# Second normalisation of a hybrid encoder step: the inverse root applied by VectorE at the take-out of the up-projection, matmuls on x times the norm's weights

## The chip, the core and the metric

The kernel runs on one core of a Trainium2 chip. The metric is the device time of one execution in microseconds, the median of several runs. A core has TensorE (PE), VectorE (DVE), ScalarE (ACT), GpSimd (POOL) and SyncE (SP, which issues the DMAs here). Each engine works through its own instruction list in order, and the lists meet only in semaphores: `wait_ge(s, n)` holds an engine until the semaphore `s` has reached `n`.

## What is computed

Two layers of an encoder for 1024 prompt positions and 32 sample positions (together T = 1056 columns), model width 1024. The attention half of a layer is not touched by the change. The half that matters is:

```python
x = x + o @ w["w_o"]
y, new["conv"] = _conv_ffn(_rms(x, w["norm2_g"]), prev, w["f_win"], w["f_conv_w"], w["f_conv_b"], w["f_wout"])
return x + y, new

def _rms(x, g):
    y = x * lax.rsqrt(jnp.mean(x * x, axis=-1, keepdims=True) + EPS)
    return y * g

def _conv_ffn(h, prev, w_in, cw, cb, w_out):     # w_in: 1024 x 5632, w_out: 2816 x 1024
    up = jnp.concatenate([prev, h @ w_in], axis=1)
    c = cb + up[:, 0:S] * cw[0]
    for j in range(1, CONV_W):                    # CONV_W = 3
        c = c + up[:, j:j + S] * cw[j]
    a, b = jnp.split(c, 2, axis=-1)
    return (jax.nn.silu(a) * b) @ w_out, up[:, S:]
```

The inverse root is one number per position. Since the up-projection is linear, it can be multiplied in before the matmul or behind it, ahead of the convolution.

## The kernel before

x lies transposed in SBUF: `x_t` is 128 partitions by 8 blocks (KC) by 1056 positions. Every large matmul is done in three parts of reduced precision: an operand is split into a high part (a cast, ScalarE) and a low part (the difference, VectorE), and `dense` (L1568) issues high x high, high x low and low x high, each over three bands of 352 positions in three PSUM banks: nine matmuls for one block of weights.

`ffn_block` begins with the second norm. `sumsq` (sums of squares over the blocks) is there already. TensorE turns it into means over the partitions (`norm.mean`, three bands, L302), ScalarE takes the roots (`norm.roots`, L308), VectorE the reciprocals (`norm.inverses`, L314). Then, for each of the 8 blocks, VectorE computes `h = x * weight * rinv` (L333), ScalarE its high part `h_hi` (L319), and VectorE or, for three blocks, GpSimd the low part `h_lo` (L324). TensorE's first two units of the up-projection run jointly along with this, block by block, as `h_lo` comes (`norm.wait_low`).

The rest is a software pipeline over i = 0 to 10 (FG = 11), four up-projection units j = 0 to 3 for each i (8 blocks x 9 matmuls = 72 matmuls each; two units for the half a and two for the half b), and behind them the down-projection `down(i)` of the pass before (8 chunks m of 18 matmuls), which adds to x. i = 0 has no down-projection, and `down(11)` follows at the end alone. The order on each engine is written out by hand in its `body`:

- TensorE: units j = 0 to 3, then `down`. A unit waits for its weights' low part (`lo_done`) and for its banks (`up_copied`). `down` waits for the low part of the second of its two weight tiles, unit number (i, 5).
- ScalarE: for each j, `ahead(i, j, split)` (the cast of the weights two units on, L1969), then `chunk`: four copies take unit j out of PSUM into `up` (L1980 to L1983, one of them puts the saved state in), and one activation begins the convolution in `cv` (L1987). For odd j follow `gate` (Silu, L1993) and `high` (cast of the product, L2001).
- VectorE: for each j, `ahead(i, j, split)` (the low part of the weights two units on, L2042), then `conv` (two instructions, L2048 and L2051), for odd j `multiply` (L2060, L2061) and `low` (L2066), and the eight adds of the down-projection to x (L2072), some of them between these.
- GpSimd saves the last two columns of each unit (L1865), and SP loads the weights (L1838), each load when the split two before it is done.

`ahead` decides what stands where: with six weight tiles (i, 0) to (i, 5) per pass it takes, at step j, the tile j + 2. So `ahead(i, 3, split)` is the split of tile (i, 5), and `ahead(i, 4)` and `ahead(i, 5)` are those of tiles (i + 1, 0) and (i + 1, 1).

Of the kernel before, what the change touches and what calls it, by code (L numbers as in the profile page):

```python
# [23 lines left out]
P = 128  # L24
# [20 lines left out]
def build_program(nc, I, O, consts):  # L45
# [71 lines left out]
    def sem(name):  # L117
        all_sems.append(nc.alloc_semaphore(name))
        return all_sems[-1]

    class S:
# [69 lines left out]
        down_done = sem("down_done")  # L191
        x_added = sem("x_added")
        st_saved = sem("st_saved")
        x_ready = sem("x_ready")
        x_sq = sem("x_sq")
        h_ready = sem("h_ready")
# [1570 lines left out]
    def ffn_block(layer):  # L1767
# [11 lines left out]
        cv = w.take("cv", [P, 2, UPC - 2])  # L1779
        up_flat = up[:, :, :].rearrange("p b c -> p (b c)")  # L1780
        sq = up_flat[:, 0:2 * T].rearrange("p (b c) -> p b c", c=T)
        w = Region(R_V + 4 * T, R_W)
        prod = w.take("prod", [P, T])
        st_t = w.take("st_t", [2 * FC * 2, 2, P])
        norm = Norm(2 * 2 * FC + 8, (6, 7, 5), Region(R_Q, R_V))
        w_sem = (S.w_loaded0, S.w_loaded1)
        win = I["f_win"][layer].rearrange("(k p) (s m c) -> s m p k c", p=P, s=2, c=P)
        wout = I["f_wout"][layer].rearrange("(m p) n -> m p n", p=P)
# [36 lines left out]
        with nc.Block() as block:  # L1825
# [29 lines left out]
            @block.gpsimd  # L1855
            def _(pool):
                pool.memset(up[:, :, 0:2], 0.0).then_inc(S.pool_step, 1)
                norm.pool_low(pool)

                def save(i):  # L1860
                    for q in range(4):
                        c = (q % 2) * FC + 2 * i + q // 2
                        pool.wait_ge(S.up_copied, 4 * i + q + 1)
                        src = up[:, q % 2, SEQ:SEQ + 68].rearrange("p (a b) -> p a b", b=34)[:, :, 0:2]
                        pool.tensor_copy(conv_st[:, :, :, bass.ds(c, 1)], src.unsqueeze(3)).then_inc(S.st_saved, 1)  # L1865

                save(0)
                with pool.Fori(1, FG) as i:
                    save(i)

            @block.tensor
            def _(pe):
                def up_unit(i, j):
                    n, ws, _ = number(i, j)
                    pe.wait_ge(S.lo_done, n + 1)
                    first = kind(i) == "first"

                    if j < 2:
                        if not first:
                            pe.wait_ge(S.up_copied, 4 * i - 1 + j)  # L1880
                            if not (isinstance(i, int) and i == 1):
                                pe.wait_ge(S.x_added, 8 * i - 9 + j)
                    else:
                        pe.wait_ge(S.up_copied, 4 * i + j - 1)
                    for k in range(KC):
                        last = dense(pe, w_hi[:, ws, k * P:(k + 1) * P], w_lo[:, ws, k * P:(k + 1) * P], k, k == 0, k == KC - 1,
                                     h_hi[:, k, :], h_lo[:, k, :], 3 * (j % 2))
                    last.then_inc(S.up_done, 1)

                def down(i, par):  # L1890

                    pe.wait_ge(S.act_lo, 2 * i)
                    for j in (4, 5):
                        n, _, _ = number(i, j)
                    pe.wait_ge(S.lo_done, n + 1)
                    for m in range(KC):
                        if m < 2:
                            if not (isinstance(i, int) and i == FG):
                                pe.wait_ge(S.up_copied, 4 * i + 3 + m)
                            else:  # L1900
                                pe.wait_ge(S.up_copied, 4 * FG - 1 + m)
                                pe.wait_ge(S.x_added, 8 * (FG - 1) - 1 + m)
                        else:
                            pe.wait_ge(S.x_added, 8 * (i - 1) + m - 1)
                        for k in range(2):
                            ws = number(i, 4 + k)[1]
                            last = dense(pe, w_hi[:, ws, m * P:(m + 1) * P], w_lo[:, ws, m * P:(m + 1) * P], k, k == 0, k == 1,
                                         act_hi[:, par, k, :], act_lo[:, par, k, :], 3 * (m % 2))
                        last.then_inc(S.down_done, 1)

                def body(i, par):
                    for j in range(2 if kind(i) == "first" else 0, 4):
                        up_unit(i, j)
                    if kind(i) != "first":
                        down(i, 1 - par)


                norm.mean(pe)
                pe.wait_ge(S.lo_done, 2)
                for k in range(KC):  # L1920
                    norm.wait_low(pe, k)
                    for j in range(2):
                        last = dense(pe, w_hi[:, j, k * P:(k + 1) * P], w_lo[:, j, k * P:(k + 1) * P], k, k == 0, k == KC - 1,
                                     h_hi[:, k, :], h_lo[:, k, :], 3 * j)
                        if k == KC - 1:
                            last.then_inc(S.up_done, 1)
                body(0, 0)
                body(1, 1)
                body(2, 0)
                with pe.Fori(1, (FG - 1) // 2) as pair:  # L1930
                    body(2 * pair + 1, 1)
                    body(2 * pair + 2, 0)
                down(FG, 0)
                for half in range(2):
                    if half == 0:
                        pe.wait_ge(S.st_saved, 4 * FG)
                    last = pe.transpose(ps[0:4 * FC, 6 + half, 0:P], conv_st[:, half, :, :].rearrange("p r c -> p (r c)"), ident[:, :])
                last.then_inc(S.tr_done, 1)

            @block.scalar  # L1940
            def _(act):
# [29 lines left out]
                def chunk(i, j):  # L1971

                    b = j % 2
                    s0 = 3 * b
                    c = b * FC + 2 * i + j // 2
                    act.wait_ge(S.up_done, 4 * i + j + 1)
                    if not (kind(i) == "first" and j < 2):
                        act.wait_ge(S.conv_done, 4 * i + j - 1)
                        act.wait_ge(S.st_saved, 4 * i + j - 1)
                    act.copy(up[:, b, 2:2 + 2 * BAND].rearrange("p (t c) -> p t c", c=BAND), ps[:, s0:s0 + 2, 0:BAND])  # L1980
                    act.copy(up[:, b, 2 + 2 * BAND:2 + SEQ], ps[:, s0 + 2, 0:SEQ - 2 * BAND])
                    act.copy(up[:, b, SEQ + 2:SEQ + 4], cols[:, 2, 0:4 * FC].rearrange("p (r c) -> p r c", c=2 * FC)[:, :, bass.ds(c, 1)].rearrange("p r c -> p (r c)"))
                    act.copy(up[:, b, SEQ + 4:UPC], ps[:, s0 + 2, SEQ - 2 * BAND:BAND]).then_inc(S.up_copied, 1)  # L1983
                    act.wait_ge(S.up_copied, 4 * i + j + 1)
                    if not (kind(i) == "first" and j < 2):
                        act.wait_ge(S.prod_done, 2 * i + j // 2)
                    act.activation(cv[:, b, :], up[:, b, 2:UPC], ACT.Identity, scale=cols[:, 1, bass.ds(c, 1)],  # L1987
                                   bias=cols[:, 1, bass.ds(c + 2 * FC, 1)]).then_inc(S.conv_init, 1)
# [22 lines left out]
                        ahead(i, 4, split)  # L2011
                        ahead(i, 5, split)

                norm.roots(act)
                split(0, 0)
                split(0, 1)
                for k in range(KC):
                    norm.high(act, k)
                body(0, 0)
                body(1, 1)  # L2020
                body(2, 0)
# [16 lines left out]
            def _(dve):  # L2038
                def split(i, j):
                    n, ws, sg = number(i, j)  # L2040
                    dve.wait_ge(S.hi_done, n + 1)
                    dve.tensor_tensor(w_lo[:, ws, :], stage[:, sg, :], w_hi[:, ws, :].bitcast(F32), ALU.subtract).then_inc(S.lo_done, 1)  # L2042

                def conv(i, j):
                    b = j % 2
# [27 lines left out]

                def body(i, par):
                    for j in range(4):
                        ahead(i, j, split)

                        if j == 3 and kind(i) != "first":
                            add(i, 0)
                        conv(i, j)  # L2080
                        if j == 3 and kind(i) != "first":
                            add(i, 1)
                        if j % 2:
                            multiply(i, j)
                            if j == 3 and kind(i) != "first":
                                add(i, 2)
                            low(i, par, j)
# [4 lines left out]
                            add(i, m)  # L2092
                        ahead(i, 5, split)

                norm.inverses(dve)
                split(0, 0)
                split(0, 1)
                norm.scaled(dve)
                body(0, 0)
                body(1, 1)  # L2100
                body(2, 0)
# [109 lines left out]
```

## Time and profile before

| | us |
|---|---|
| median of 3 runs | 3335.66 (3333.11 to 3339.05) |
| profiled execution | 3342.06 |
| its span | 3340.3 |
| TensorE matmuls busy | 2934.7 |
| VectorE busy | 1788.4 |
| ScalarE busy | 1333.8 |
| mean granted clock of TensorE | 0.933 |

In the profile PE is TensorE's matmuls and PEld its weight loads, which overlap them. A row of the timeline gives start, duration, engine, line and operation, out<-in with the shape, how many instructions are merged, and in brackets the idle time of the engine ahead of it with what ended that. A granted clock of 1.00 is TensorE's upper level (2.4 GHz), 0.50 the lower (1.2 GHz). The feed-forward blocks of the two layers lie at 872 to 1672 us and 2517 to 3317 us.

### The profile page before, as it was taken

Reading aid. Unit: us, or ns where it says so; the run is one execution under the profiler, and the core shown is the slowest. Engines: PE = TensorE matmul, PEld = TensorE weight load, DVE = VectorE, ACT = ScalarE, POOL = GpSimd, SP = SyncE. Lnnn points to the kernel's source line nnn. Section 1 sums busy time; section 2 is a strip of 40 time slices with the busy share of each in tenths; the row PEclk is TensorE's granted clock in tenths of the full one; section 3 lists DMA queues with packets and bytes.
Section 4 is the critical chain, followed back from the end, with each engine's and each line's share of the span. In section 5 each row is a group of like instructions: output and inputs, shape, how many; then the busy total and the mean of one; then the engine's idle time right before and its main releaser. Section 6 shows DMA issues by size and latency. Waiting matters only on the chain. (4 is left out here: it accounts for less than half of the span.)

```text
span 3340.3 us, 49479 instructions
## 1 busy us (share of the span) xinstructions
PE 2934.7 (88%) x19032; PEld 2721.1 (81%) x19032; DVE 1788.4 (54%) x2837; ACT 1333.8 (40%) x2759; POOL 164.7 (5%) x238
## 2 busy tenths in 40 slices
PE   5887788788899999999968877788898999999997
PEld 3785677478799999999957756676687999999997
DVE  5467664755554444544565586566436444544444
ACT  5557653542232233222245574455413332222233
POOL 0200011000000000000002000120001000000000
PEclk8898889798899999999978998797898999999999
DMA  4110101013111111111031101200301111111111
GB/s 173 51 39 15 33 13 53 8 47 117 32 51 51 45 39 51 39 48 48 20 121 58 34 10 32 51 16 9 135 26 51 49 41 51 39 45 51 45 45 60
DMA packets 185835, 162.17 MB, mean 49 GB/s; under 512 B 17272, under 2 KB 172408, under 8 KB 185080
## 3 DMA queue, kind: packets, MB, share of 16 engines
q1 hardware_dynamic: 185592, 158.82, 15.2%
q8 instruction: 167, 2.74, 0.3%
q14 instruction: 76, 0.62, 0.1%
HBM read 129.92 MB, written 29.06 MB: 48 GB/s over the span
## 5 line engine op out<-in xcount | busy, mean ns | idle before, releaser
L1568 PE MATMUL ps<-h_hi,w_hi 128*128 128x352 f32 x2496 | 546.0, 327 | 50.8 <-DVE h_lo L324 22.6
L1568 PE MATMUL ps<-h_hi,w_lo 128*128 128x352 f32 x2496 | 541.3, 324 | 0.0
L1568 PE MATMUL ps<-h_lo,w_hi 128*128 128x352 f32 x2496 | 541.3, 325 | 0.0
L1568 PEld LDWEIGHTS ps<-h_hi,w_hi 128*128 128x128 f32 x2496 | 428.4, 191 | 58.3 <-issue 44.0
L1568 PEld LDWEIGHTS ps<-h_hi,w_lo 128*128 128x128 f32 x2496 | 431.6, 189 | 0.0
L1568 PEld LDWEIGHTS ps<-h_lo,w_hi 128*128 128x128 f32 x2496 | 428.1, 189 | 0.0
L725 PE MATMUL ps<-w_hi,h_hi 128*128 128x256 f32 (+1 forms) x1152 | 337.2, 293 | 69.1 <-DVE w_lo L890 65.0
L2072 DVE TENSOR_TENSOR x_t<-ps,x_t 128x1056 f32<-128x1056 f32 x176 | 221.1, 1256 | 289.5 <-PE ps L1568 288.8
L2048 DVE SCALAR_TENSOR_TENSOR cv<-up,cols,cv 128x1058 f32<-128x1058 f32 x88 | 116.1, 1319 | 478.1 <-ACT cv L1987 478.1
L726 PE MATMUL ps<-w_lo,h_hi 128*128 128x256 f32 (+1 forms) x1152 | 332.6, 289 | 0.0
L727 PE MATMUL ps<-w_hi,h_lo 128*128 128x256 f32 (+1 forms) x1152 | 330.3, 287 | 0.0
L1980 ACT COPY up<-ps 128x704 f32<-128x704 f32 x88 | 65.7, 747 | 591.8 <-PE ps L1568 591.8
L725 PEld LDWEIGHTS ps<-w_hi,h_hi 128*128 128x128 f32 (+1 forms) x1152 | 215.1, 187 | 73.7 <-DVE w_lo L890 48.9
L1305 ACT ACTIVATE prob<-ps,nm 128x256 f32<-128x256 f32 (+8 forms) x360 | 224.9, 639 | 55.7 <-DVE nm L1221 45.4
L1568 PE MATMUL ps<-act_hi,w_hi 128*128 128x352 f32 x1056 | 229.5, 325 | 5.1 <-issue 5.1
L1969 ACT CAST w_hi<-stage 128x1024 fp32r<-128x1024 f32 x132 | 136.0, 1043 | 241.4 <-PE ps L1568 240.8
L1568 PE MATMUL ps<-act_lo,w_hi 128*128 128x352 f32 x1056 | 228.9, 325 | 0.0
L1568 PE MATMUL ps<-act_hi,w_lo 128*128 128x352 f32 x1056 | 228.5, 324 | 0.0
L727 PEld LDWEIGHTS ps<-w_hi,h_lo 128*128 128x128 f32 (+1 forms) x1152 | 215.8, 187 | 0.9
L726 PEld LDWEIGHTS ps<-w_lo,h_hi 128*128 128x128 f32 (+1 forms) x1152 | 214.8, 186 | 0.8
L1221 DVE TENSOR_REDUCE nm<-ps 128x1 f32<-128x128 f32 (+10 forms) x234 | 184.4, 788 | 27.9 <-PE ps L1133 16.1
L1142 PE MATMUL ps<-k_st,q_st 96*128 96x512 f32 (+7 forms) x480 | 143.9, 418 | 47.2 <-ACT prob L1305 39.2
(200 smaller groups left out, 4413.5 us busy)
## 6 DMA issues: line engine op xcount, KB each, us to landing
stage<-in_f_win SPq DMA_DIRECT2D x88, 512.0 KB, 3.8
stage<-in_f_wout SPq DMA_DIRECT2D x44, 512.0 KB, 3.7
stage<-in_w_in SPq DMA_DIRECT2D x64, 256.0 KB, 3.9
x_spill<-x_t SPq DMA_DIRECT2D x2, 4224.0 KB, 14.1
o_in<-o_spill SPq DMA_DIRECT2D x8, 1056.0 KB, 10.1
x_t<-x_spill SPq DMA_DIRECT2D x2, 4224.0 KB
stage<-in_w_o SPq DMA_DIRECT2D x16, 512.0 KB, 5.9
x_in<-in_x_prompt SPq DMA_DIRECT2D x1, 4096.0 KB, 13.6
```

What stands on the lines that cost most here:

```text
L725: pe.matmul(out, h_hi[:, k, c:c + r], w_hi[:, k, :], start=(k == 0), stop=False)
L726: pe.matmul(out, h_hi[:, k, c:c + r], w_lo[:, k, :], start=False, stop=False)
L727: last = pe.matmul(out, h_lo[:, k, c:c + r], w_hi[:, k, :], start=False, stop=(k == KC - 1))
L1142: last = pe.matmul(out, q_st[0:nk, qb, q0:q0 + r], jb["k"][0:nk, jb["k_blk"] + kb, k0 + c:k0 + c + n], start=(m == 0), stop=(m == len(pair ...
L1221: dve.tensor_reduce(nm[0:r, j % 4, 0:nh], v, AX.X, ALU.max, negate=True).then_inc(S.nm_done, 1)
L1305: last = act.activation(prob[0:r, j % 4, col:col + kn], src, ACT.Exp, bias=nm[0:r, j % 4, i:i + 1], accum_out=rsum[0:r, j % 4, i:i + 1])
L1568: last = pe.matmul(ps[:, s0 + b, 0:BAND], lh, rh_[:, b * BAND:(b + 1) * BAND], start=(first_k and n == 0), stop=(last_k and n == 2))
L1969: act.copy(w_hi[:, ws, :], stage[:, sg, :]).then_inc(S.hi_done, 1)
L1980: act.copy(up[:, b, 2:2 + 2 * BAND].rearrange("p (t c) -> p t c", c=BAND), ps[:, s0:s0 + 2, 0:BAND])
L2048: dve.scalar_tensor_tensor(cv[:, b, :], up[:, b, 1:UPC - 1], cols[:, 0, bass.ds(c + 2 * FC, 1)], cv[:, b, :], ALU.mult, ALU.add).then_inc( ...
L2072: dve.tensor_tensor(xm, ps[:, s0:s0 + 3, 0:BAND], xm, ALU.add).then_inc(S.x_added, 1)
```

## The change

The norm's inverse root is no longer multiplied into the matmul's operand. ScalarE makes `h_hi` from x times the weight column (`high_x`), VectorE makes `h_lo` with the same product less `h_hi` (`low_x`); GpSimd makes none. The root is written to `rinv` and inverted there by one reciprocal. `take_up` is new: VectorE multiplies each up-projection unit by `rinv` as it takes it out of PSUM into `up`, in three instructions, in place of ScalarE's three copies out of PSUM. ScalarE keeps the small copy of the saved state and waits for `up_copied`. The third mean stands behind the first two blocks of the joint units on TensorE, in bank 6. In VectorE's `body`, `take_up(i, j)` stands ahead of `ahead(i, j, split)`.

```diff
@@ -1779,10 +1780,12 @@
         cv = w.take("cv", [P, 2, UPC - 2])
         up_flat = up[:, :, :].rearrange("p b c -> p (b c)")
         sq = up_flat[:, 0:2 * T].rearrange("p (b c) -> p b c", c=T)
+        st_t = w.take("st_t", [2 * FC * 2, 2, P])
         w = Region(R_V + 4 * T, R_W)
         prod = w.take("prod", [P, T])
-        st_t = w.take("st_t", [2 * FC * 2, 2, P])
-        norm = Norm(2 * 2 * FC + 8, (6, 7, 5), Region(R_Q, R_V))
+        rinv = w.take("rinv", [P, T])
+        gain0 = 2 * 2 * FC + 8
+        mean_banks = (6, 7, 6)
         w_sem = (S.w_loaded0, S.w_loaded1)
         win = I["f_win"][layer].rearrange("(k p) (s m c) -> s m p k c", p=P, s=2, c=P)
         wout = I["f_wout"][layer].rearrange("(m p) n -> m p n", p=P)
@@ -1855,7 +1858,6 @@
             @block.gpsimd
             def _(pool):
                 pool.memset(up[:, :, 0:2], 0.0).then_inc(S.pool_step, 1)
-                norm.pool_low(pool)
 
                 def save(i):
                     for q in range(4):
@@ -1915,10 +1917,18 @@
                         down(i, 1 - par)
 
 
-                norm.mean(pe)
+                def mean(b):
+                    pe.matmul(ps[:, mean_banks[b], 0:BAND], mean_w[:, :], sumsq[:, b * BAND:(b + 1) * BAND],
+                              start=True, stop=True).then_inc(S.norm_mean, 1)
+
+                mean(0)
+                mean(1)
                 pe.wait_ge(S.lo_done, 2)
                 for k in range(KC):
-                    norm.wait_low(pe, k)
+                    pe.wait_ge(S.norm_lo, k + 1)
+                    if k == 2:
+                        pe.wait_ge(S.norm_root, 1)
+                        mean(2)
                     for j in range(2):
                         last = dense(pe, w_hi[:, j, k * P:(k + 1) * P], w_lo[:, j, k * P:(k + 1) * P], k, k == 0, k == KC - 1,
                                      h_hi[:, k, :], h_lo[:, k, :], 3 * j)
@@ -1973,14 +1983,11 @@
                     b = j % 2
                     s0 = 3 * b
                     c = b * FC + 2 * i + j // 2
-                    act.wait_ge(S.up_done, 4 * i + j + 1)
                     if not (kind(i) == "first" and j < 2):
                         act.wait_ge(S.conv_done, 4 * i + j - 1)
-                        act.wait_ge(S.st_saved, 4 * i + j - 1)
-                    act.copy(up[:, b, 2:2 + 2 * BAND].rearrange("p (t c) -> p t c", c=BAND), ps[:, s0:s0 + 2, 0:BAND])
-                    act.copy(up[:, b, 2 + 2 * BAND:2 + SEQ], ps[:, s0 + 2, 0:SEQ - 2 * BAND])
-                    act.copy(up[:, b, SEQ + 2:SEQ + 4], cols[:, 2, 0:4 * FC].rearrange("p (r c) -> p r c", c=2 * FC)[:, :, bass.ds(c, 1)].rearrange("p r c -> p (r c)"))
-                    act.copy(up[:, b, SEQ + 4:UPC], ps[:, s0 + 2, SEQ - 2 * BAND:BAND]).then_inc(S.up_copied, 1)
+                    act.copy(up[:, b, SEQ + 2:SEQ + 4], cols[:, 2, 0:4 * FC].rearrange("p (r c) -> p r c", c=2 * FC)[:, :, bass.ds(c, 1)].rearrange("p r c -> p (r c)")
+                             ).then_inc(S.st_in, 1)
+                    act.wait_ge(S.st_in, 4 * i + j + 1)
                     act.wait_ge(S.up_copied, 4 * i + j + 1)
                     if not (kind(i) == "first" and j < 2):
                         act.wait_ge(S.prod_done, 2 * i + j // 2)
@@ -2011,11 +2018,23 @@
                         ahead(i, 4, split)
                         ahead(i, 5, split)
 
-                norm.roots(act)
+                def high_x(k):
+                    act.mul(h_hi[:, k, :], x_t[:, k, :], cols[:, 0, gain0 + k:gain0 + k + 1]).then_inc(S.norm_hi, 1)
+
+                def root(b):
+                    act.wait_ge(S.norm_mean, b + 1)
+                    act.activation(rinv[:, b * BAND:(b + 1) * BAND], ps[:, mean_banks[b], 0:BAND], ACT.Sqrt,
+                                   bias=eps_c[:, 0:1]).then_inc(S.norm_root, 1)
+
+                high_x(0)
                 split(0, 0)
                 split(0, 1)
-                for k in range(KC):
-                    norm.high(act, k)
+                high_x(1)
+                root(0)
+                root(1)
+                for k in range(2, KC):
+                    high_x(k)
+                root(2)
                 body(0, 0)
                 body(1, 1)
                 body(2, 0)
@@ -2041,6 +2060,20 @@
                     dve.wait_ge(S.hi_done, n + 1)
                     dve.tensor_tensor(w_lo[:, ws, :], stage[:, sg, :], w_hi[:, ws, :].bitcast(F32), ALU.subtract).then_inc(S.lo_done, 1)
 
+                def take_up(i, j):
+
+                    b = j % 2
+                    s0 = 3 * b
+                    dve.wait_ge(S.up_done, 4 * i + j + 1)
+                    if not (kind(i) == "first" and j < 2):
+                        dve.wait_ge(S.conv_done, 4 * i + j - 1)
+                        dve.wait_ge(S.st_saved, 4 * i + j - 1)
+                    dve.tensor_tensor(up[:, b, 2:2 + 2 * BAND].rearrange("p (t c) -> p t c", c=BAND), ps[:, s0:s0 + 2, 0:BAND],
+                                      rinv[:, 0:2 * BAND].rearrange("p (t c) -> p t c", c=BAND), ALU.mult)
+                    dve.tensor_tensor(up[:, b, 2 + 2 * BAND:2 + SEQ], ps[:, s0 + 2, 0:SEQ - 2 * BAND], rinv[:, 2 * BAND:SEQ], ALU.mult)
+                    dve.tensor_tensor(up[:, b, SEQ + 4:UPC], ps[:, s0 + 2, SEQ - 2 * BAND:BAND], rinv[:, SEQ:T], ALU.mult
+                                      ).then_inc(S.up_copied, 1)
+
                 def conv(i, j):
                     b = j % 2
                     c = b * FC + 2 * i + j // 2
@@ -2073,6 +2106,7 @@
 
                 def body(i, par):
                     for j in range(4):
+                        take_up(i, j)
                         ahead(i, j, split)
 
                         if j == 3 and kind(i) != "first":
@@ -2092,10 +2126,19 @@
                             add(i, m)
                         ahead(i, 5, split)
 
-                norm.inverses(dve)
+                def low_x(k):
+                    dve.wait_ge(S.norm_hi, k + 1)
+                    dve.scalar_tensor_tensor(h_lo[:, k, :], x_t[:, k, :], cols[:, 0, gain0 + k:gain0 + k + 1],
+                                             h_hi[:, k, :].bitcast(F32), ALU.mult, ALU.subtract).then_inc(S.norm_lo, 1)
+
+                low_x(0)
                 split(0, 0)
                 split(0, 1)
-                norm.scaled(dve)
+                for k in range(1, KC):
+                    low_x(k)
+                dve.wait_ge(S.norm_root, BANDS)
+                dve.reciprocal(rinv[:, :], rinv[:, :]).then_inc(S.norm_inv, 1)
+                dve.wait_ge(S.norm_inv, 1)
                 body(0, 0)
                 body(1, 1)
                 body(2, 0)
```

## Rows read from the trace of the kernel before

**Rows 1.** The page: busy time, share of the span and instructions of each engine.

```profile
PE 2934.7 (88%) x19032; PEld 2721.1 (81%) x19032; DVE 1788.4 (54%) x2837; ACT 1333.8 (40%) x2759; POOL 164.7 (5%) x238
```

**Rows 2.** Table of stretches: length, then busy time of each engine, clock, DMA.

```profile
core 0: us, PE busy (x) PEld busy (x) DVE busy (x) ACT busy (x) POOL busy (x), PEclk, DMA share, GB/s
872.50:887.70 15.20, 3.86 (x6) 1.86 (x7) 12.79 (x9) 5.78 (x7) 0.22 (x2) 0.50 0.48 136
887.70:891.40 3.70, 3.68 (x13) 3.70 (x14) 3.70 (x2) 0.23 (x1) 2.32 (x1) 0.50 0.03 10
...
1088.00:1158.00 70.00, 70.00 (x434) 70.00 (x433) 32.20 (x28) 20.00 (x30) 0.77 (x4) 1.00 0.15 46
```

**Rows 3.** Timeline of the first block's head, all engines.

```profile
872.57 3.86 PE L302 MATMUL ps<-sumsq,mean_w 128*128 128x352 f32 x6 [4.94 <-PEq L203]
...
874.77 6.78 DVE L314 RECIPROCAL rinv<-root 128x352 f32<-128x352 f32 x3 [3.32 <-ACT root L308]
...
876.92 1.03 ACT L1969 CAST w_hi<-stage 128x1024 fp32r<-128x1024 f32 x1
878.31 1.04 ACT L1969 CAST w_hi<-stage 128x1024 fp32r<-128x1024 f32 x1 [0.36 <-DMA stage<-in_f_win]
...
887.72 1.22 PE L1568 MATMUL ps<-h_hi,w_hi 128*128 128x352 f32 x3 [11.29 <-DVE h_lo L324]
```

**Rows 4.** Groups of instructions of 872 to 1672 us: count, busy, mean, idle before.

```profile
L2072 DVE TENSOR_TENSOR x_t<-ps,x_t 128x1056 f32<-128x1056 f32 x88 | 110.5, 1256 | 144.8 <-PE ps L1568 144.4
...
L2042 DVE TENSOR_TENSOR w_lo<-stage,w_hi 128x1024 fp32r<-128x1024 f32 x66 | 79.5, 1218 | 0.0
...
L2061 DVE TENSOR_TENSOR prod<-cv 128x32 f32<-128x32 f32 x22 | 4.0, 184 | 0.0
```

**Rows 5.** Timeline of the first layer's last down-projection, where TensorE runs dry.

```profile
1640.72 1.22 DVE L2042 TENSOR_TENSOR w_lo<-stage,w_hi 128x1024 fp32r<-128x1024 f32 x1
...
1642.04 0.78 PE L1568 MATMUL ps<-act_hi,w_hi 128*128 128x352 f32 x3 [2.53 <-issue]
1646.76 1.26 DVE L2072 TENSOR_TENSOR x_t<-ps,x_t 128x1056 f32<-128x1056 f32 x1 [4.82 <-PE ps L1568]
```

**Rows 6.** Timeline of ScalarE at the same place.

```profile
1122.92 0.75 ACT L1980 COPY up<-ps 128x704 f32<-128x704 f32 x1 [8.02 <-PE ps L1568]
...
1123.97 0.20 ACT L1983 COPY up<-ps 128x32 f32<-128x32 f32 x1
```

**Rows 7.** Timeline of VectorE around it.

```profile
1116.81 1.22 DVE L2042 TENSOR_TENSOR w_lo<-stage,w_hi 128x1024 fp32r<-128x1024 f32 x1
1125.83 1.26 DVE L2072 TENSOR_TENSOR x_t<-ps,x_t 128x1056 f32<-128x1056 f32 x1 [7.81 <-PE ps L1568]
```

**Rows 8.** Timeline of TensorE, from up-projection unit 3 to the down-projection.

```profile
1122.24 0.65 PE L1568 MATMUL ps<-h_hi,w_lo 128*128 128x352 f32 x3
1122.72 0.65 PE L1568 MATMUL ps<-act_hi,w_hi 128*128 128x352 f32 x3
```

**Rows 9.** Table of stretches without a matmul, and right behind such ones.

```profile
1642.60:1646.00 3.40, 3.40 (x14) 3.40 (x13) 0.00 (x0) 0.00 (x0) 0.00 (x0) 0.50 0.00 0
187.60:190.00 2.40, 0.00 (x0) 0.00 (x0) 2.37 (x6) 2.40 (x5) 0.00 (x0) 1.00 0.00 0
190.10:195.00 4.90, 4.90 (x41) 4.90 (x42) 4.79 (x11) 0.59 (x2) 0.00 (x0) 1.00 0.67 205
432.40:435.80 3.40, 0.00 (x0) 0.03 (x1) 3.33 (x7) 2.79 (x6) 0.00 (x0) 1.00 0.00 0
435.90:440.00 4.10, 4.10 (x35) 4.10 (x36) 4.00 (x11) 0.30 (x1) 0.00 (x0) 1.00 0.06 16
2237.60:2240.20 2.60, 0.00 (x0) 0.00 (x0) 1.76 (x5) 1.82 (x7) 0.00 (x0) 0.94 0.00 0
2240.30:2245.00 4.70, 4.70 (x10) 1.82 (x11) 4.23 (x16) 3.31 (x12) 0.00 (x0) 0.50 0.02 4
...
3287.80:3291.20 3.40, 3.40 (x13) 3.40 (x12) 0.00 (x0) 0.00 (x0) 0.00 (x0) 0.50 0.00 0
```

More of the change, by code:

```diff
@@ L193, in build_program @@
         st_saved = sem("st_saved")
+        st_in = sem("st_in")
         x_ready = sem("x_ready")
```

## Prediction

> **What bounds the kernel now.** I read the page first: TensorE is busy for 88% of the span and no other engine comes near [rows 1]. Then the table of stretches, to see which part of it the change touches. In the feed-forward loop TensorE is busy for 70.00 of 70.00 us of one pass (1088 to 1158 us), at the full granted clock, while VectorE works 32.2 us and ScalarE 20.0 us of the same pass [rows 2]. So in the loop only TensorE's own stream counts: whatever VectorE does there is free as long as nobody makes TensorE wait, and every microsecond of such a wait is added in full. At the head of the block it is the other way round: from 872.5 to 887.7 us TensorE is busy for 3.86 of 15.2 us while VectorE is busy for 12.8 [rows 2]. There the chain over VectorE sets the start of the matmuls. Both layers run the same code (the same place comes 1645.2 us later, as 1642.6 and 3287.8 in rows 9 show), so every term counts twice.
>
> **The head: what is removed.** Before, the chain is: mean matmuls, roots, three reciprocals, the two weight splits, the first scaled x, its high part, its low part, first matmul at 887.72 [rows 3]. In the change the first matmul needs only x times a weight (its high part on ScalarE, its low part on VectorE, both of which can run while the first weights are still loading) and the two weight splits. Those hang on the transfers: ScalarE's first cast is at 876.92, the second waits for its DMA until 878.31 and takes 1.04 us, so it ends at 879.35; VectorE's split of it is 1.22 us [rows 3, 4], and TensorE starts 0.10 us behind a split (1640.72 + 1.22 to 1642.04 in rows 5). That gives 879.35 + 0.05 + 1.22 + 0.10 = 880.7 in place of 887.72: 7.0 us less. TensorE ran the first 3.7 us of its stream at half clock [rows 2]; in the new order it will have been idle for some 5.5 us ahead of it (two of three means end near 875.1), so I count the same loss.
>
> **The head: what is added.** (a) The third mean moves from the idle time into the matmul stream, ahead of the third k. Six such matmuls take 3.86 us at half clock [rows 2, 3], so two take 1.29 us, and about half of that, 0.65, at full clock: 1.0 us taken. (b) The other high and low parts (near to the 1.04 and 1.22 us of the weights' cast and split, rows 3 and 4) outrun TensorE, which needs 18 matmuls, 2.9 us, for each k. The reciprocal of 1056 columns (three of 352 took 6.78 us, rows 3) would begin near 890 and end near 897. It is needed when the first up-projections are done, near 905: covered, by about 8 us; if that cover went, what is over would be on the path. (c) After the joint k loop TensorE begins the third unit when unit 0 has been taken out and the weights of the third unit are split. VectorE's split of those weights now stands behind `take_up(0, 0)` in its queue. By the prices worked out below it is done 2.53 us after the take-out begins, and unit 0 is complete 1.46 us (nine matmuls) before TensorE's stream runs dry. So the new wait is 0.20 + 2.53 + 0.10 - 1.46 = 1.4 us, where the old one was about 0.1: 1.3 us more. Sum for one head: -7.0 + 1.0 + 1.3 = -4.7 us, twice -9.4 us.
>
> **The loop: the take-out itself.** Four ScalarE copies become three VectorE multiplications. VectorE's price by rows: 1056 columns with a PSUM operand 1256 ns, 32 columns in SBUF 184 ns [rows 4]; slope (1256 - 184) / 1024 = 1.047 ns a column. So 704, 320 and 32 columns are 888, 486 and 184 ns; an instruction starts some 0.08 us before the one ahead is recorded as ended, so together 1.31 us. No row shows the multiplication with these access patterns. Its bounds are the 1.25 us which ScalarE's copies take now (the first at 1122.92, rows 6, the last ended at 1124.17, same rows) and 1.6 us (three parts without the overlap); I take 1.31, since the 1256 ns row has the same operation class, type and bank-crossing operand. VectorE's load per pass rises from 32.2 to 37.4 us of 70: no bound. Between two units VectorE has 11.66 us (72 matmuls of 0.162 us); its fullest such stretch becomes take-out 1.3, split 1.2, convolution 2.7, product 1.4, wait for the high part 1.1, low part 1.3, with ScalarE's 1.3 us before the convolution: about 9.5 us. It fits with 2 us over.
>
> **The loop: what is moved behind a wait.** This decides it. VectorE's `body` now begins each j with `take_up(i, j)`, which waits for the end of up-projection unit j, and only then does `ahead(i, j, split)`, the split of the weights two units on. For j = 0, 1, 2 the result is needed a whole unit later: hidden by 11.66 - 2.5 us. For j = 3 it is the split of unit (i, 5), the second down-projection weight, and `down(i)` on TensorE begins right at the end of unit 3 and waits for exactly this `lo_done`. Before, this split ran at 1116.81, six microseconds before unit 3 ended [rows 7]; TensorE went over from unit 3 to the down-projection without a break at 1122.72 [rows 8], and ScalarE began to take unit 3 out at 1122.92 [rows 6], 0.20 us later. Now: VectorE starts the take-out at +0.20, its three instructions 1.31, the split 1.22, TensorE released +0.10: a stall of 2.83, say 2.85 us with the extra register waits in the loop. Queued behind the waiting take-out on VectorE are also the adds and the convolution, but these wait for the down-projection or for ScalarE anyway and shift with it. SP's next weight load (it waits for `lo_done`) comes later too, with over 10 us in hand. The stall occurs for i = 1 to 10, 20 times in all: 20 x 2.85 = 57.0 us. `down(11)` already has its own stall of this kind and keeps it.
>
> **The clock after the stall.** That old stall is the nearest row. At 1639.5 TensorE ran dry, waited 2.53 us for the split at 1640.72, restarted at 1642.04 [rows 5], and the granted clock was then 0.50 (the 1.2 GHz level) from 1642.6 to 1646.0, and likewise in the second layer at 3287.8 [rows 9]. The first eighteen matmuls took until the add at 1646.76, 4.72 us, against 3.11 (from 1122.72 to the add at 1125.83, rows 7, 8): 1.6 us more. Not every gap does this. After 2.4 us (187.6 to 190.0) and after 3.4 us (432.4 to 435.8) without a matmul the clock stayed at 1.00, after 2.6 us (2237.6) it fell to 0.50 [rows 9]. Bounds for 20 stalls: 0 and 32 us. Three of the five fell, and the likest two are among them: I take 12 of 20, 12 x 1.6 = 19.2 us.
>
> **Rule against row.** The Trainium skill (TensorE: Matmul & The Clock Gate, HAM oscillation) warns of idle gaps that are longer than the 2.7 us which I expect; by its rule these stalls would cost no clock at all. The two gaps after which the clock stayed up agree with it, the three others don't. By the rule the sum would be smaller by the 19.2 us; it is the first rival.
>
> **The sum.** -9.4 + 57.0 + 19.2 = +66.8 us. The profiled execution took 3342.06 us (span 3340.3 and 1.8 around it) and would become 3409; it lies 6.4 us above the median of 3335.66, and the terms don't depend on that. Forecast: 3335.66 + 66.8 = 3402.5 us.
>
> **Rivals.**
> 1. The stalls, but at full clock: 3335.66 - 9.4 + 57.0 = 3383 us. For it: two gaps without a fall. Against it: the same place in the same loop falls in both layers.
> 2. The other side: the late split makes nobody wait, and only the head counts: 3335.66 - 9.4 = 3326 us, faster. It would need the split of (i, 5) done before unit 3's last matmul, that is, no longer queued behind the take-out, which begins only 0.20 us after that matmul. It decides in TensorE's favour only if the split ends 2.8 us earlier than I read the queue order. Against it: the order stands in the code, and `down` names this count. For it: only that no trace shows the new order.
> 3. VectorE as a second brake: if the take-out costs twice what I say (2.6 us), each stall grows by 1.3 us and the stretch between units nearly fills its 11.66 us: 3402.5 + 20 x 1.3 = 3428 us. For it: no row has a multiplication with this mixed pattern. Against it: the 1256 ns row.
> 4. That the change doesn't do what it says (the inverse root late for the first take-out) would show as a wait at the head; it is covered by 8 us and worth at most a few microseconds.
>
> **How the numbers follow.** Forecast case 0.77 (its own range 3390 to 3416: from 4 to all 20 stalls with the fall), rival 1 0.11, rival 2 0.04, rival 3 0.07, rest 0.01. The range goes down to rival 1 with a take-out at ScalarE's pace, 3378, and up to all stalls with the fall and a take-out of 1.6 us, 3415 + 6 = 3421, with a little for rival 3: 3424. A measurement of this kernel can tell 0.2%, some 7 us, from no change: faster 0.04, same 0.02, slower 0.94.
>
> **What the new profile would show.** First matmul of the block near +8 us after its start, not +15. In each pass of 70 us: the split of (i, 5) right behind three multiplications on VectorE, TensorE idle for about 2.7 us before its first `act_hi` matmul, released by VectorE's `w_lo`, and often a granted clock of 0.50 right after it; the pass grows to 73 to 75 us. VectorE's busy time rises by about 88 x 1.5 us less the reciprocals and scalings. If TensorE's idle time before `act_hi` stays at 5 us in total, the central step is wrong; if there are 20 gaps without a low clock, the clock term is.

## The result

The changed kernel takes 3412.2 us (median of 4 runs, 3408.8 to 3413.1) against 3337.4 us (4 runs, 3333.1 to 3340.7): slower by the factor 1.0222, interval 1.0206 to 1.0238. Forecast were 3402.5 us and a range of 3378 to 3424 us. The profiled execution took 3411.97 us, span 3410.1 us, 69.9 us more than the one of before.

From the page of the changed kernel, the busy times and, of the costliest groups, the first matmuls on `act_hi`. The last part of a group's row is the engine's idle time just before these instructions and what ended most of it:

```profile
PE 2961.6 (87%) x19032; PEld 2744.1 (80%) x19032; DVE 1884.8 (55%) x3087; ACT 1232.4 (36%) x2495; POOL 222.7 (7%) x232
...
L1569 PE MATMUL ps<-act_hi,w_hi 128*128 128x352 f32 x1056 | 241.5, 339 | 58.7 <-DVE w_lo L2061 43.0
```

The same group in the kernel before:

```profile
L1568 PE MATMUL ps<-act_hi,w_hi 128*128 128x352 f32 x1056 | 229.5, 325 | 5.1 <-issue 5.1
```

VectorE has 96 us more to do and ScalarE 101 us less (against rows 1), and by the runs below neither matters. What matters is in the group's row: TensorE stood still for 58.7 us ahead of the down-projections, where it was 5.1 us. For 43.0 us of it the row names what was waited for, the low part of weights, `w_lo`. In addition these matmuls are slower themselves, 339 ns in the mean where they took 325 ns.

The place is the change-over from up-projection unit 3 to the down-projection, the one of rows 6, 7 and 8. The timeline of the changed kernel, VectorE first:

```profile
1125.04 0.89 DVE L2071 TENSOR_TENSOR up<-ps,rinv 128x704 f32<-128x704 f32 x1 [5.85 <-PE ps L1569]
1125.85 0.48 DVE L2073 TENSOR_TENSOR up<-ps,rinv 128x320 f32<-128x320 f32 x1
1126.25 0.18 DVE L2074 TENSOR_TENSOR up<-ps,rinv 128x32 f32<-128x32 f32 x1
1126.35 1.22 DVE L2061 TENSOR_TENSOR w_lo<-stage,w_hi 128x1024 fp32r<-128x1024 f32 x1
1132.39 1.26 DVE L2105 TENSOR_TENSOR x_t<-ps,x_t 128x1056 f32<-128x1056 f32 x1 [4.83 <-PE ps L1569]
```

and TensorE:

```profile
1124.35 0.65 PE L1569 MATMUL ps<-h_hi,w_lo 128*128 128x352 f32 x3
1127.69 0.74 PE L1569 MATMUL ps<-act_hi,w_hi 128*128 128x352 f32 x3 [2.69 <-DVE w_lo L2061]
```

The three multiplications and the split behind them take 1125.04 to 1127.57, and TensorE goes on 0.12 us later. Its stream would have gone on at 1124.84 (three matmuls of 0.162 us after 1124.35), so the stall is 2.85 us. (The row's own idle time, 2.69 us, is smaller, because a matmul is recorded as ended 0.16 us after the next one could have started.) There are 20 such stalls. Behind 16 of them the view names `w_lo`; behind the first two of each layer it says "issue" (no cause that the profile shows), with 2.66 us of idle time and the same four VectorE instructions in it. Before, the same change-over had no break at all [rows 8]. The first add of the down-projection comes 4.70 us after the restart where it was 3.11 us: the granted clock has fallen. The table of stretches, of 4 us behind each of the first layer's ten waits (columns as in rows 2; the last but two is the granted clock):

```profile
979.30:983.30 4.00, 4.00 (x17) 4.00 (x18) 0.00 (x0) 1.04 (x2) 0.00 (x0) 0.65 0.44 131
1053.40:1057.40 4.00, 4.00 (x16) 4.00 (x17) 0.00 (x0) 1.03 (x2) 0.00 (x0) 0.57 0.44 131
1127.70:1131.70 4.00, 4.00 (x17) 4.00 (x18) 0.00 (x0) 1.19 (x2) 0.00 (x0) 0.65 0.46 134
1202.10:1206.10 4.00, 4.00 (x25) 4.00 (x26) 0.85 (x1) 1.14 (x2) 0.00 (x0) 1.00 0.44 131
1276.40:1280.40 4.00, 4.00 (x14) 4.00 (x15) 0.00 (x0) 1.13 (x2) 0.00 (x0) 0.50 0.48 134
1352.00:1356.00 4.00, 4.00 (x25) 4.00 (x26) 0.90 (x1) 1.13 (x2) 0.00 (x0) 1.00 0.45 131
1426.10:1430.10 4.00, 4.00 (x16) 4.00 (x17) 0.00 (x0) 1.15 (x2) 0.00 (x0) 0.61 0.47 134
1500.40:1504.40 4.00, 4.00 (x16) 4.00 (x17) 0.00 (x0) 1.15 (x2) 0.00 (x0) 0.57 0.44 131
1576.20:1580.20 4.00, 4.00 (x16) 4.00 (x17) 0.00 (x0) 0.99 (x2) 0.00 (x0) 0.60 0.46 131
1650.50:1654.50 4.00, 4.00 (x16) 4.00 (x17) 0.00 (x0) 1.03 (x2) 0.00 (x0) 0.58 0.46 131
```

Behind eight of the ten waits the clock fell, and 14 to 17 matmuls were done in 4 us where 25 are done at full clock: nine fewer, or 1.5 us. The second layer has nine of ten. So 17 of the 20 waits were followed by a fall.

The head, against rows 3 (TensorE, ScalarE, VectorE and GpSimd mixed, as the timeline has them):

```profile
871.51 2.68 PE L1921 MATMUL ps<-sumsq,mean_w 128*128 128x352 f32 x4 [4.98 <-PEq L204]
...
877.15 1.04 ACT L1979 CAST w_hi<-stage 128x1024 fp32r<-128x1024 f32 x1 [0.61 <-DMA stage<-in_f_win]
...
878.23 1.23 DVE L2061 TENSOR_TENSOR w_lo<-stage,w_hi 128x1024 fp32r<-128x1024 f32 x1 [0.43 <-ACT w_hi L1979]
...
879.51 1.25 PE L1569 MATMUL ps<-h_hi,w_hi 128*128 128x352 f32 x3 [5.32 <-DVE w_lo L2061]
...
887.06 0.75 PE L1921 MATMUL ps<-sumsq,mean_w 128*128 128x352 f32 x2
887.38 0.91 PE L1569 MATMUL ps<-h_hi,w_hi 128*128 128x352 f32 x3
...
888.65 6.74 DVE L2140 RECIPROCAL rinv<-rinv 128x1056 f32<-128x1056 f32 x1
...
903.84 0.89 DVE L2071 TENSOR_TENSOR up<-ps,rinv 128x704 f32<-128x704 f32 x1 [8.45 <-PE ps L1569]
...
906.41 0.74 PE L1569 MATMUL ps<-h_hi,w_hi 128*128 128x352 f32 x3 [1.22 <-DVE w_lo L2061]
```

From the first mean to the first matmul of the up-projection it is 8.00 us, not 15.15. From there to the third unit it is 26.90 us, not 25.16: the third mean, 0.6 us, and a wait of 1.2 us for a split behind a take-out. In sum 5.4 us less in this layer; in the second the same two numbers are 8.14 and 27.09, 5.1 us less.

Laid out over the two layers, from the two traces: heads -10.5 us, 20 stalls of 2.85 us +57.0 us, and what the ten passes of each layer are longer beyond that, the clock, +27.9 us (they take 748.3 and 748.1 us from the first matmul of unit (1, 0) to that of `down(11)`, where it was 705.8 and 705.7). Together +74.4 us, and measured, between the medians, are +74.8. The two profiled executions themselves differ by 69.9 us, because the rest of the kernel, which the change doesn't touch, took 4.5 us less in the second; the profiled execution of before lay 4.7 us above its median.

### The profile page after: what moved, and what is told of

The parts are those of the page before. It is cut to its first block and busy times, and to the rows that moved or that the text cites. A ratio compares the mean times of both kernels' runs of the same rounds, so it can differ in the third digit from the quotient of the medians.

```text
span 3410.1 us, 49447 instructions
## 1 busy us (share of the span) xinstructions
PE 2961.6 (87%) x19032; PEld 2744.1 (80%) x19032; DVE 1884.8 (55%) x3087; ACT 1232.4 (36%) x2495; POOL 222.7 (7%) x232
## 5 line engine op out<-in xcount | busy, mean ns | idle before, releaser
L1994 ACT ACTIVATE cv<-up,cols 128x1058 f32<-128x1058 f32 x88 | 112.1, 1274 | 728.7 <-issue 690.8
L2071 DVE TENSOR_TENSOR up<-ps,rinv 128x704 f32<-128x704 f32 x88 | 78.5, 892 | 490.3 <-PE ps L1569 490.3
L1569 PE MATMUL ps<-act_hi,w_hi 128*128 128x352 f32 x1056 | 241.5, 339 | 58.7 <-DVE w_lo L2061 43.0
L726 PEld LDWEIGHTS ps<-w_hi,h_hi 128*128 128x128 f32 (+1 forms) x1152 | 214.4, 186 | 74.4 <-DVE w_lo L891 49.4
L1569 PEld LDWEIGHTS ps<-act_hi,w_hi 128*128 128x128 f32 x1056 | 189.3, 200 | 64.8 <-issue 64.8
L1569 PE MATMUL ps<-act_lo,w_hi 128*128 128x352 f32 x1056 | 238.5, 336 | 0.0
L1569 PE MATMUL ps<-act_hi,w_lo 128*128 128x352 f32 x1056 | 237.5, 334 | 0.0
```

What stands on the lines that cost most here:

```text
L726: pe.matmul(out, h_hi[:, k, c:c + r], w_hi[:, k, :], start=(k == 0), stop=False)
L1569: last = pe.matmul(ps[:, s0 + b, 0:BAND], lh, rh_[:, b * BAND:(b + 1) * BAND], start=(first_k and n == 0), stop=(last_k and n == 2))
L2071: dve.tensor_tensor(up[:, b, 2:2 + 2 * BAND].rearrange("p (t c) -> p t c", c=BAND), ps[:, s0:s0 + 2, 0:BAND], rinv[:, 0:2 * BAND].rearrang ...
```

## The experiments

Theory A is the prediction's: the loss comes from the order on VectorE, with the split of tile (i, 5) queued behind a take-out that waits for the end of unit 3. Theory B says that the take-out on VectorE costs by itself, by its load or by reading PSUM while TensorE writes it. Beside them stands the question whether the clock is a term of its own.

**The split first, for every j.**

```diff
                     for j in range(4):
-                        take_up(i, j)
                         ahead(i, j, split)
+                        take_up(i, j)
```

> VectorE's body does the split of the weights two units on before the take-out, for every j; nothing else changes. Theory A (the queue order makes the loss: the split of tile (i, 5) stands behind a take-out that waits for the end of unit 3): all 20 gaps of 2.69 us ahead of the down-projection go, and the 1.2 us ahead of the third unit at each head too; only the shorter heads are left, 3337 - 2 x 6.6 = 3324 us. Theory B (the take-out itself costs, since VectorE has 5 us more work per pass and reads PSUM while TensorE writes it): the order changes little, 3380 us or more.

Measured: 3326.6 us against 3339.2 of the kernel before on the same chip, ratio 0.9954 (0.9939 to 0.997). It is faster than the kernel before. The same change-over, VectorE and then TensorE:

```profile
1114.95 1.22 DVE L2061 TENSOR_TENSOR w_lo<-stage,w_hi 128x1024 fp32r<-128x1024 f32 x1
1120.88 0.89 DVE L2071 TENSOR_TENSOR up<-ps,rinv 128x704 f32<-128x704 f32 x1 [4.71 <-PE ps L1569]
```

```profile
1120.20 0.65 PE L1569 MATMUL ps<-h_hi,w_lo 128*128 128x352 f32 x3
1120.68 0.65 PE L1569 MATMUL ps<-act_hi,w_hi 128*128 128x352 f32 x3
```

The split is done 4.5 us before unit 3 ends, TensorE goes over without a break, and the take-out is the same instruction at the same 0.89 us. The loss hung on two lines' order. Theory A holds, B falls. (That the figure meets the 3326 us of the prediction's second rival is luck; see below.)

**The split first for j = 3 alone.**

```diff
                     for j in range(4):
+                        if j == 3:
+                            ahead(i, j, split)
                         take_up(i, j)
-                        ahead(i, j, split)
+                        if j != 3:
+                            ahead(i, j, split)
```

> The order is swapped for j = 3 only. Theory A: the 20 gaps go, the wait of 1.2 us ahead of the third unit at each head stays: 3324 + 2.4 = 3326.5 us. Theory B: 3380 us or more. A rival inside A, that the later splits for j = 0, 1, 2 cost something in each pass too: then it is slower than the kernel with all four swapped by more than 2.4 us.

Measured: 3326.2 us, ratio 0.9964 (0.9953 to 0.9976). The wait ahead of the third unit is there in each head (1.23 us in the trace), but its 2.4 us are less than the spread of the runs, and the two kernels can't be told apart. What can be said: j = 3 carries all of the loss in the loop (without it TensorE's passes take 69.92 us, as before), and the late splits of the other three cost nothing that shows.

**The take-out back on ScalarE.**

```diff
 def chunk(i, j):                                # ScalarE
+    act.wait_ge(S.up_done, 4 * i + j + 1)
+    act.copy(up[:, b, 2:2 + 2 * BAND]..., ps[:, s0:s0 + 2, 0:BAND])
...
 def body(i, par):                               # VectorE
     for j in range(4):
-        take_up(i, j)
         ahead(i, j, split)
```

> The changed kernel's head, but the take-out of the up-projection goes back to ScalarE's copies as before, without the multiplication by the inverse root (this part of the computation is left out: the output is that of a norm without its root). VectorE's body begins with the split again. Theory A (only the place of the split counts): the same as with the split first and VectorE's take-out, 3326 us within 3, and the wait ahead of the third unit is 0.1 us. Theory B (VectorE's take-out costs something beside the order, by its load or by reading PSUM): faster than that kernel by more than 3 us.

Measured: 3326.2 us, ratio 0.9961 (0.9948 to 0.9973). This kernel leaves the multiplication by the inverse root out. Within the some 5 us that the intervals leave open it takes the same time as with VectorE's take-out and the split first (0.9954). So once the split is out of its way, the 5 us more per pass on VectorE are free, as its idle time in rows 2 said.

**The wait alone, in the kernel before.**

```diff
                     for j in range(4):
+                        if j == 3:
+                            dve.wait_ge(S.up_done, 4 * i + 4)
                         ahead(i, j, split)
```

> The kernel before with one thing added: at j = 3 VectorE waits for the end of unit 3 before it splits tile (i, 5). Norm, take-out by ScalarE and all else as before. Theory A: a wait of 0.20 + 1.22 + 0.10 = 1.5 us ahead of each down-projection, 20 x 1.5 = 30 us: 3337 + 30 = 3367 us, more only where the clock falls (not expected after gaps of 1.4 us; if it falls each time, 3399 us). Theory B (the loss comes from the take-out): no change, 3337 us.

Measured: 3374.4 us against 3339.2, ratio 1.0099 (1.0083 to 1.0116), +35 us where 30 were expected. Without norm, take-out or anything else of the change, one added wait makes almost half the loss. The trace of one change-over, ScalarE, VectorE and TensorE:

```profile
1127.04 0.75 ACT L1980 COPY up<-ps 128x704 f32<-128x704 f32 x1 [8.03 <-PE ps L1568]
1127.48 1.23 DVE L2042 TENSOR_TENSOR w_lo<-stage,w_hi 128x1024 fp32r<-128x1024 f32 x1 [6.47 <-PE ps L1568]
...
1128.83 0.74 PE L1568 MATMUL ps<-act_hi,w_hi 128*128 128x352 f32 x3 [1.83 <-DVE w_lo L2042]
```

Here VectorE begins 0.44 us later than ScalarE, which waits for the same end of unit 3, so this wait is 2.0 us and not 1.5; others in the trace show idle times of 1.4 to 1.8 us. Why VectorE is later in some passes stays open. The granted clock stayed at 1.00 behind all of them: none of the 20 gaps of 1.4 to 1.8 us was followed by a fall.

**TensorE kept busy during the wait.**

```diff
+                    if not (isinstance(i, int) and i == FG):
+                        for _ in range(15):
+                            pe.matmul(ps[:, 7, 0:BAND], h_hi[:, 0, 0:P], h_hi[:, 0, 0:BAND], start=True, stop=True)
                     pe.wait_ge(S.lo_done, n + 1)
```

> The order of the changed kernel is kept, and with it the wait; TensorE does 15 matmuls of 352 columns (2.44 us) on data that nobody reads, in an unused bank, ahead of each of the 20 waits. The idle time of 2.69 us becomes some 0.3 us, the restart comes at the same moment. Theory A with the clock as a term of its own: the 17 falls of the granted clock behind these gaps go, each worth 1.6 us: 3412 - 28 = 3384 us, and each pass is 72.8 us. If the clock's part is the 12 x 1.6 = 19 us of the prediction, 3393 us. If the low clock has nothing to do with the idle time: 3412 us.

Measured: 3403.4 us, ratio 1.0188 (1.0171 to 1.0205): 19 us too many for the first theory, and not the 3412 of the other. The trace says why. In the passes 1 to 3 of each layer (counted from one down-projection to the next) only some 0.3 us of idle time are left and the clock stays up; they take 72.8 us, 69.92 + 2.85. But in every second pass of the later ones TensorE has a new break in the first matmuls of unit (i, 0), where the loop's code starts anew:

```profile
1224.44 0.74 PE L1569 MATMUL ps<-h_hi,w_hi 128*128 128x352 f32 x3 [0.76 <-issue]
...
1227.29 0.66 PE L1569 MATMUL ps<-h_lo,w_hi 128*128 128x352 f32 x1 [1.79 <-issue]
```

and the clock falls behind that one instead (table of stretches: the break, and what follows):

```profile
1225.50:1227.30 1.80, 0.01 (x2) 0.01 (x1) 0.61 (x1) 0.31 (x2) 0.00 (x0) 0.99 0.00 0
1227.30:1230.60 3.30, 3.30 (x11) 3.30 (x12) 0.00 (x0) 0.00 (x0) 0.00 (x0) 0.50 0.57 164
```

There are six such passes, three in each layer. They take 77.2 to 79.3 us, where the same passes of the next kernel take 73.9 to 74.4; in sum that is 21.9 us, so these breaks and the falls behind them account for the excess. The filler is 30 instructions more in each pass, which pointed to the length of the stream. So the next kernel has as much filling in fewer instructions.

```diff
-                        for _ in range(15):
-                            pe.matmul(ps[:, 7, 0:BAND], h_hi[:, 0, 0:P], h_hi[:, 0, 0:BAND], start=True, stop=True)
+                        for _ in range(8):
+                            pe.matmul(ps[:, 7, 0:512], h_hi[:, 0, 0:P], h_hi[:, 0, 0:512], start=True, stop=True)
```

> As the filler before, with 8 matmuls of 512 columns (1.7 us) in place of 15 of 352, so with half the added instructions. The filler with 15 removed the falls behind the 20 waits but had breaks of 1 to 2 us and low clocks in the first matmuls of every second pass. If these came from the longer instruction stream, they shrink here: passes of 72.8 us, and towards 3384 us in all. If they come from the missing idle time itself, they stay, 3403 us. If 1.0 us of idle time that is left is enough for the clock to fall, passes of 74.3 us and 3412 us.

Measured: 3386.3 us against 3339.5, ratio 1.0134 (1.0119 to 1.015). The timeline of a change-over and the 4 us behind it:

```profile
1122.46 1.99 PE L1899 MATMUL ps<-h_hi 128*128 128x512 f32 x8
1125.30 0.75 PE L1569 MATMUL ps<-act_hi,w_hi 128*128 128x352 f32 x3 [0.86 <-DVE w_lo L2064]
```

```profile
1125.30:1129.30 4.00, 4.00 (x25) 4.00 (x26) 0.79 (x1) 1.21 (x2) 0.00 (x0) 1.00 0.44 131
```

The down-projection still begins only when the split is done, passes without a loop edge take 72.8 to 72.9 us, and behind none of the 20 waits the clock falls. That parts the loss in two on the chip: 46.8 us remain without the falls (57.0 - 10.5 = 46.5 by the layout above), and 74.8 - 46.8 = 28 us are the clock, to some 7 us by the intervals; the layout from the traces gave 27.9. The new breaks inside unit (i, 0) are gone too; that they come from the number of instructions is what this pair of kernels suggests, not what it shows, for the width of the matmuls changed as well.

**Two steps on from the version with every split first.** The first lets TensorE begin unit 0 on the first block when the first weight tile is split; the second fills the idle time ahead of it.

```diff
-                pe.wait_ge(S.lo_done, 2)
+                pe.wait_ge(S.norm_hi, 1)          # the second version alone
+                for _ in range(11):               # the second version alone
+                    pe.matmul(ps[:, 5, 0:BAND], h_hi[:, 0, 0:P], h_hi[:, 0, 0:BAND], start=True, stop=True)
+                pe.wait_ge(S.lo_done, 1)
                 for k in range(KC):
...
                     for j in range(2):
+                        if k == 0 and j == 1:
+                            pe.wait_ge(S.lo_done, 2)
```

> The kernel with all four splits first, and at the head TensorE starts unit 0 on the first block when the first weight tile is split, and waits for the second only ahead of unit 1. By the rows of the changed kernel the first split ends at 877.81 us, the second at 879.46: start 1.65 us earlier, nine cold matmuls (2.6 us) cover the second. 3326.6 - 2 x 1.65 = 3323.3 us; no gain if the clock rises later by as much.

> The same, with 11 matmuls of 352 columns on data that nobody reads between the second mean and the first block, where TensorE is idle for 5.3 us, to have the clock up sooner. In the changed kernel the first 3.6 us of the stream run at half clock and lose 1.7 us. If activity ahead of the stream raises the clock, up to 2 x 1.7 us less: 3320 us. If not, 3323 us.

Measured: 3324.1 us (0.995, 0.9936 to 0.9963) and 3320.7 us (0.9941, 0.9928 to 0.9955), beside 3326.6 (0.9954) without either. The intervals overlap, so the sizes of the steps have to be read from the traces. From the first mean to the third unit of the first layer it is 34.13 us without either, 33.26 us in the first version and 30.87 us in the second. Together that is the 3.3 us for each head that was expected, but the first step gave 0.87 us of its 1.65. Its stream starts 6.4 us after the first mean instead of 8.1, and the clock comes up no sooner, 12.4 us after the first mean against 12.3: what was gained at the start ran at the low clock. Its table of stretches, from the first matmul on:

```profile
882.80:886.80 4.00, 4.00 (x14) 4.00 (x15) 3.06 (x3) 4.00 (x6) 0.00 (x0) 0.50 0.55 159
886.80:890.80 4.00, 4.00 (x21) 4.00 (x20) 4.00 (x4) 4.00 (x5) 0.00 (x0) 0.75 0.36 107
```

The second step gave the rest, 2.39 us. The timeline of TensorE in the second version and its table of stretches:

```profile
874.50 3.74 PE L1928 MATMUL ps<-h_hi 128*128 128x352 f32 x11
...
879.05 0.76 PE L1569 MATMUL ps<-h_hi,w_hi 128*128 128x352 f32 x3 [0.81 <-DVE w_lo L2066]
```

```profile
879.00:882.00 3.00, 2.95 (x17) 2.74 (x18) 2.46 (x2) 3.00 (x5) 0.00 (x0) 1.00 0.50 149
```

The real stream begins 6.5 us after the first mean and at once at full clock, where that of the changed kernel ran its first 3.5 us at 0.50. This version is 0.6% faster than the kernel before and 2.7% faster than the changed one (0.9941 / 1.0222 = 0.9725).

## Why the prediction was right, point by point

- **What bounds.** Right. TensorE's stream is the only thing that counts in the loop; VectorE's 5 us more per pass are free as long as nobody waits (the take-out back on ScalarE made no difference), and each microsecond of a wait is added in full.
- **The head, removed.** 7.0 us forecast, 7.15 and 7.0 us measured, by the same chain: the second transfer, cast, split, start.
- **The head, added.** The third mean was taken at 1.0 us and cost some 0.6 (0.5 in the first layer and 0.7 in the second remain beside the wait), the full-clock end of its bounds, since the clock was up at 887 us. The wait ahead of the third unit was 1.2 us of idle time for 1.3 forecast. The reciprocal ended at 895.4, over 8 us before its use. Sum: -4.7 forecast per head, -5.4 and -5.1 measured.
- **The take-out.** 888, 486 and 184 ns forecast, 892, 481 and 181 ns in the trace.
- **The split behind a wait.** 20 stalls of 2.85 us forecast; 20 of 2.82 to 2.85 us measured, with `w_lo` named behind 16 and the same instructions in the other four. Swapping the two lines took all of them away.
- **The clock.** The mechanism was right and the number was short: 12 falls of 1.6 us, 19.2 us, against 17 falls and 28 us. This term is what parts the forecast, +66.8, from the measured +74.8 (of the 9.7 us between 3402.5 and 3412.2 another 1.7 are the base, 3335.66 against 3337.4). The step that was off is the choice of the rate. It was drawn from five gaps, and the two without a fall among them lie in quite other stages (rows 9), while the gap of the same form and place (rows 5) was followed by a fall in both layers. More gaps of other stages wouldn't have helped: with three more of the same trace (at 224.8 us, then 1.00; at 261.3, then 0.50; at 758.8, then 0.54) it is five falls of eight, the same rate. The gap that comes is 2.69 us, a little longer than that row's 2.53, and that row alone would have said 20 of 20, 32 us, or 3415 us. The measured 17 lies nearer to it. But that row isn't certain either. Every kernel of this document has the gap of 2.53 us in both layers, and it was followed by a fall in 18 of 20 cases. Here is one of the two without, the 4 us behind the first layer's gap in the version with the earlier unit:

```profile
1638.10:1642.10 4.00, 4.00 (x25) 4.00 (x26) 0.92 (x1) 0.00 (x0) 0.00 (x0) 1.00 0.00 0
```

- **Rule against row.** The rule of the Trainium skill (TensorE: Matmul & The Clock Gate, HAM oscillation) would have idle gaps of this length cost no clock, and the sum 3383 us. 17 of 20 gaps of 2.66 to 2.69 us did cost it, so here the measurement decides against the rule as it is worded. For the gaps of 1.4 to 1.8 us ahead of `down(i)` (the wait alone) the trace agrees with it; for the six breaks of 1.5 to 2.1 us in the kernel with 15 fillers, each with a fall behind it, it doesn't. The prediction counted both gaps without a fall for the rule. The one ending at 435.8 us was 3.48 us long, no shorter than the gaps that the rule warns of, so only the other speaks for it.
- **The rivals.** The faster side, 3326 us, would have needed the split out of the take-out's way, and with just that edit the loss was gone: 3326.6 us. That the two figures meet is luck: the rival is 9.4 us below a base of 3335.66, the run 12.5 us below 3339.2, mainly since swapping all four splits also took the new wait ahead of the third unit away. VectorE as a second brake didn't happen.
- **Two slips in the sums.** The fullest stretch of VectorE between two units was given as 9.5 us; its terms add up to 10.3, which still fits into 11.66. The lower end of the range, 3378 us, was explained by rival 1 with a take-out at ScalarE's pace; 20 times 0.06 us less than 3383 is 3382. Neither changes the forecast.

## What to carry to other kernels

When work moves to another engine, read not only whether that engine has time, but what stands behind the moved piece in its queue: a take-out that waits for the end of a matmul group holds back everything that was there to run ahead of that end. Put the look-ahead work (splits, loads, casts for the next unit) ahead of the first instruction that waits for the present unit. And price a stall on TensorE with what its clock costs afterwards: here a wait of 2.85 us cost 4.2 us.

## What the hardware showed beyond the forecast

- A gap without matmuls of 2.66 to 2.69 us was followed by a granted clock of 0.50 in 17 of 20 cases and by none in three, with the same instructions ahead and behind. With 1.4 to 1.8 us ahead of the same matmuls it was 0 of 20, yet in the kernel with 15 fillers a break of 1.79 us was followed by a fall, with another of 0.76 us about a microsecond ahead of it. So were the other five breaks of that kind in this kernel, of 1.5 to 2.1 us. And the gap of 2.53 us in each layer's last down-projection had no fall behind it in two of 20 cases. So the length of one gap doesn't decide alone.
- Matmuls on data that nobody reads, put into a wait, kept the clock up behind it (25 matmuls in 4 us, not 16) and, in the head, raised it before the real stream began.
- TensorE's stream has breaks of its own of 0.7 to 1.4 us at the loop's edge, for most of which the profile names nothing to wait for. They were there in the kernel before as well (0.9 to 1.1 us; its passes 4, 6 and 8 take 71 us, not 70). When 30 instructions were added to each pass, a second break of 1.5 to 2.1 us came behind each of them, with a fall of the clock behind it. What sets them stays open.
